# Expert layer of a small diffusion backbone: the last tile of the GLU product taken weight by weight, and the ring handed over unit by unit

## Chip, cores and metric

The kernel runs on one core of one Trainium2 chip. The metric is the device time of one execution in microseconds (us); the median of several executions is compared. All operands are fp32.

## What is computed

One layer (DEPTH is 1) for 128 context tokens and 256 latent tokens of width 1024, three tiles of 128 tokens. Cut to what the change touches:

```python
# ssm_mixer, its end: y is (tokens, 1024), w_glu is (1024, 2048)
val, gate = jnp.split(jax.nn.gelu(y).astype(h.dtype) @ w_glu, 2, axis=-1)
m = val * jax.nn.sigmoid(gate)
# run_stream
x = x + g1 * m
h = rms_norm(x, p["norm_ffn"][i]) * (1 + sc2) + sh2
# moe: router of 16 experts, best group of 4, two best experts in it
scores = jax.nn.sigmoid((t @ router_w).astype(jnp.float32))
g = jnp.einsum("nd,edf->nef", t, w_gate)
u = jnp.einsum("nd,edf->nef", t, w_up)
a = jax.nn.silu(g) * u * combine[:, :, None].astype(t.dtype)
y = jnp.einsum("nef,efd->nd", a, w_down)
x = x + g2 * moe(h, ...)        # then one final rms_norm
```

## The kernel before

The engines run five instruction lists written by hand; each keeps its own order and waits on semaphores. The list of SyncE (SP) issues nearly all DMAs.

**The ring.** The tile `ring` has 12 slots ("units") of 1 MB. Slots 0 to 7 later hold the gate and up weights of one expert (128 of the 1024 rows each), slots 8 to 11 its down weights (256 rows each). Before that, slots 4 to 11 hold `w_glu`, 128 rows in each slot (`load_glu`), slot 2 holds `yT_lat`, the transposed latent activations, and slots 0, 1 and 3 hold inputs of stages that end with the transposes counted by `pe_yT`.

**The GLU product** ("linear unit") is made in six parts m = 0 to 5 (`glu_part`, L1005): token tile t = m // 2, output half m % 2, and for each part `val` and `gate` in two PSUM banks (`GLU_BANK`). A part is 16 matmuls 128x512, which the trace shows as 32 records. Parts 0 and 1 are the context tile, 2 and 3 the first latent tile, 4 and 5 the second (last) one. Each part sums over eight slots, in the order of k = 4 to 7, then 0 to 3.

**After a part**: ScalarE takes the sigmoid (L700), VectorE multiplies, scales and adds to `x1` (L1416 to L1418), which counts `dve_x1`. After both parts of a tile ScalarE squares and sums (L707), takes a root (L709), and VectorE modulates to `h2` (L1333 to L1336). TensorE transposes `h2` (`transpose_h2`, L1040), ScalarE copies it out (`store_h2T`, L692), TensorE makes the 16 router logits of the tile (`logits`, L1049).

**Routing**: with all three tiles' logits, ScalarE takes the scores (L714) and VectorE chooses experts in some 40 small instructions (L1432 to L1495). TensorE sums ranks (L1070, L1071) and gathers the first expert's tokens (`gather_x`, L1082), VectorE copies them out (L1519, L1520).

**Experts**: a loop over 16. TensorE reads the expert's token count (L1128), branches to a body for 64 or for 96 tokens (L1129, L1131), multiplies by gate and up (L1096, a record per pass, 128 of them for 64 tokens and 192 for 96), gathers the next expert's tokens (L1082), transposes (L1108) and multiplies by down (L1118). Every slot is counted free in `unit_free` once read, and SP at once issues the same slot's load for the next expert (L368, L374). The last expert stands outside the loop. GpSimd scatters slot lists (L465) and each expert's output rows (L491).

**What sets the order around the change.** SP loads slots 0 and 1 for expert 0 after `pe_yT` 6, and then waits for all twelve counts of `pe_glu`, two per part, before it issues slots 2 to 11:

```python
            sp.wait_ge(pe_yT, 6)
            for u in range(2):
                load_unit(u, 0)
            sp.wait_ge(pe_glu, 12)
            for u in range(2, NU):
                load_unit(u, 0)
            sp.wait_ge(dve_x1, 6)
```

TensorE makes parts 2, 3 and 4, transposes tile 0 of `h2` into the two banks that part 5 then takes, waits for ScalarE's copies of it (`act_h2T` 2), and makes part 5.

Of the kernel before, what the change touches and what calls it, by code (L numbers as in the profile page):

```python
# [41 lines left out]
P = 128  # L42
D = 1024
KT = D // P
# [23 lines left out]
NU = 12  # L68
# [8 lines left out]
GLU_BANK = (2, 4, 0, 6, 2, 4)  # L77
# [4 lines left out]
def build(nc, x_prompt, x_sample, c, state_re, state_im, c_ctx, norm_mix, norm_ffn, w_ada, b_ada,  # L82
# [7 lines left out]
    with ctx:  # L90
        def sb(name, shape, dt=F32):
            return ctx.enter_context(nc.sbuf_tensor(name, shape, dt))

        def sem(name):
            return ctx.enter_context(nc.semaphore(name))


        ring = sb("ring", [P, NU, UNIT])
# [39 lines left out]
        yT_lat = ring[:, 2, :].rearrange("p (k t) -> p k t", k=KT)  # L138
# [18 lines left out]
        def cut(region, n):  # L157
            a = region[:, off[0]:off[0] + n]
            off[0] += n
            return a  # L160
        braw = cut(sreg, 2 * DG * GS).rearrange("p (r g h) -> p r g h", r=2, g=DG)
        craw = cut(sreg, 2 * DG * GS).rearrange("p (r g h) -> p r g h", r=2, g=DG)
        part = cut(sreg, GP * L * GS).rearrange("p (g k h) -> p g k h", k=L, h=GS)
# [53 lines left out]
        ps = [ctx.enter_context(nc.psum_tensor(f"ps{i}", [P, 512], F32)) for i in range(8)]  # L217
# [15 lines left out]
        pe_tr, pe_ada, pe_bc, pe_w, pe_cols, pe_hT, pe_u, pe_uT, pe_k, pe_p, pe_y, pe_fin, pe_yT = (  # L233
            sem(n) for n in ("pe_tr", "pe_ada", "pe_bc", "pe_w", "pe_cols", "pe_hT", "pe_u", "pe_uT",
                             "pe_k", "pe_p", "pe_y", "pe_fin", "pe_yT"))
        pe_inside = sem("pe_inside")
        act_ada, ld_glu_hi, ld_x_ctx, ld_mod_ctx = (sem(n) for n in ("act_ada", "ld_glu_hi", "ld_x_ctx", "ld_mod_ctx"))
        act_xs, act_lat, dve_rs, dve_cols, dve_ctx, act_v0 = (sem(n) for n in (
            "act_xs", "act_lat", "dve_rs", "dve_cols", "dve_ctx", "act_v0"))
        pe_glu, pe_h2T, pe_logit, pe_pos = (sem(n) for n in (  # L240
            "pe_glu", "pe_h2T", "pe_logit", "pe_pos"))
# [3 lines left out]
        act_yT, act_sig, act_h2T, act_score, act_fin, act_h0 = (sem(n) for n in (  # L245
            "act_yT", "act_sig", "act_h2T", "act_score", "act_fin", "act_h0"))
# [6 lines left out]
        dve_scan, dve_x1, dve_h2, dve_mask, dve_slot, dve_cmax, dve_x2, dve_out = (sem(n) for n in (  # L253
            "dve_scan", "dve_x1", "dve_h2", "dve_mask", "dve_slot", "dve_cmax", "dve_x2", "dve_out"))
# [23 lines left out]
        def of_half(i):  # L278
            return ident[:, :].rearrange("p (b i o) -> p i b o", i=2, o=2)[:, i]
# [7 lines left out]
        def _(sp):  # L287
# [23 lines left out]
            for n in range(KT, 3 * KT):  # L311
                b, k = divmod(n, KT)
# [52 lines left out]
            def load_unit(u, e):  # L365
                if u < KT:
                    for h, w in enumerate((w_gate, w_up)):
                        sp.dma_start(ring[:, u, h * D:(h + 1) * D],  # L368
                                     w[0, bass.ds(e, 1), u * P:(u + 1) * P, :].rearrange("a p n -> (a p) n")
                                     ).then_inc(ld_unit[u], 16)  # L370
                else:
                    for h in range(2):
                        k = 2 * (u - KT) + h
                        sp.dma_start(ring[:, u, h * D:(h + 1) * D],  # L374
                                     w_down[0, bass.ds(e, 1), k * P:(k + 1) * P, :].rearrange("a p n -> (a p) n")
                                     ).then_inc(ld_unit[u], 16)

            sp.wait_ge(pe_yT, 6)
            for u in range(2):
                load_unit(u, 0)  # L380
            sp.wait_ge(pe_glu, 12)
            for u in range(2, NU):
                load_unit(u, 0)
            sp.wait_ge(dve_x1, 6)
            for cond in range(2):
# [132 lines left out]
        def _(act):  # L518
# [51 lines left out]
            for m in range(2 * NT):  # L570
                t, k0 = m // 2, 4 * (m % 2)
# [116 lines left out]
            def store_h2T(t):  # L688
                for m in (2 * t, 2 * t + 1):
                    k0 = 4 * (m % 2)  # L690
                    act.wait_ge(pe_h2T, m + 1)
                    act.activation(h2T[:, k0:k0 + 4, t * P:(t + 1) * P],  # L692
                                   ps[(0 if t == 1 else 4) + m % 2][:, :].rearrange("p (k n) -> p k n", k=4), ACT.Copy
                                   ).then_inc(act_h2T, 1)
            for t in range(NT):
                for m in (2 * t, 2 * t + 1):
                    act.wait_ge(pe_glu, 2 * m + 2)
                    if m:
                        act.wait_ge(dve_x1, m)
                    act.activation(sig, ps[GLU_BANK[m] + 1][:, :], ACT.Sigmoid).then_inc(act_sig, 1)  # L700
                    if m == 4:
                        store_h2T(1)

                act.wait_ge(dve_x1, 2 * t + 2)
                if t:
                    act.wait_ge(act_sq, NT + t)
                act.activation(yrow, x1[:, t, :], ACT.Square, accum_out=stat[:, t:t + 1]).then_inc(act_sq, 1)  # L707
                act.wait_ge(dve_ms, 2 + t)
                act.activation(stat[:, 4 + t:5 + t], stat[:, 4 + t:5 + t], ACT.Sqrt).then_inc(act_rt, 1)  # L709
                if t == 1:  # L710
                    store_h2T(0)
            store_h2T(2)
            act.wait_ge(pe_logit, NT)
            act.activation(route[:, 0], ps[6][:, 0:NT * NE].rearrange("p (t e) -> p t e", t=NT), ACT.Sigmoid  # L714
# [43 lines left out]
        def _(pe):  # L758
# [20 lines left out]
            for i in range(2):  # L779
# [3 lines left out]
                for n, rows_in in enumerate((lnat[:, 0, :], lnat[:, 1, :], dtexp)):  # L783
                    last = pe.matmul(ps[7][a, n * DG:(n + 1) * DG], rows_in, of_half(i), start=True, stop=True)
# [37 lines left out]
            for i in range(2):  # L822
                last = pe.transpose(ps[3][:, 8 * i:8 * i + 8], drow[:, P * i:P * i + P], ident[0:8, 0:8])
# [8 lines left out]
            for q in range(4):  # L832
                last = pe.transpose(ps[3][:, q * P:(q + 1) * P], ada[:, 0, q * P:(q + 1) * P], ident[:])
# [46 lines left out]
            for m in range(8):  # L880
                if m >= 4:
                    pe.wait_ge(act_uT if m % 2 == 0 else dve_uT, (m - 4) // 2 + (1 if m % 2 == 0 else 2))
                for g in range(4 * m, 4 * m + 4):
                    src = u_c[0:C, 2 * g:2 * g + 2, :, :].rearrange("p i j h -> p (i j h)")
                    last = pe.transpose(ps[4 + m % 4][:, (g % 4) * C:(g % 4 + 1) * C], src, ident[0:C, 0:C])
# [6 lines left out]
            for m in range(0, 32, 2):  # L892
# [4 lines left out]
                for bi in range(2):  # L897
                    for r in range(2):
                        c0 = (2 * r + bi) * CX
                        for o in range(2):  # L900
                            a = slice(64 * o, 64 * o + 64)
                            for i in range(2):
                                g = 2 * (b0 + bi) + i
                                last = pe.matmul(ps[m % 8 + o][64 * i:64 * i + 64, c0:c0 + CX], pt[a, d, g, r, :],
                                                 uT[a, g, :], start=True, stop=True)
# [29 lines left out]
            def lat_bank(f, i):  # L935
                return ps[6 * f + i]
# [4 lines left out]
            def y_inside(bank_of, blocks, first_col, cols):  # L941
                for n, b in enumerate(blocks):
                    for i in range(2):
                        g = 2 * b + i
                        for o in range(2):
                            a = slice(64 * o, 64 * o + 64)
                            last = pe.matmul(y_out(bank_of(i), i, n, o, cols), t_of[a, g % 4, g // 4, :],
                                             uT[a, g, first_col:first_col + cols],
                                             start=(n == 0), stop=False, skip_group_check=True)
                return last  # L950
# [15 lines left out]
            def y_channels(k, bank, col, cols, y_of):  # L966
                for t in range(L):
                    for q in range(4):
                        last = pe.matmul(bank[32 * q:32 * q + 32, col + t * cols:col + (t + 1) * cols], pick[:, t, :],
                                         y_of(q % 2, 2 * k + q // 2), start=True, stop=True)  # L970
                return last
# [20 lines left out]
            for k in range(KT):  # L992
                last = y_channels(k, ps[2 + k // 4], (k % 4) * P, CC, lambda i, b: y_ctx[:, i, b, :])
# [23 lines left out]
            for f in range(2):  # L1017
                last = y_inside(lambda i: lat_bank(f, i), range(8 * f, 8 * f + 8), LAT0, CL)
# [5 lines left out]
            for f in range(2):  # L1024
                pe.wait_ge(act_gelu, 4 + 2 * f)
                for k in range(4 * f, 4 * f + 4):
                    last = y_channels(k, lat_bank(f, k % 4 // 2), (k % 2) * 256, CL,
                                      lambda i, b: y_lat[:, b // 8, i, b % 8, :])
# [4 lines left out]
            def transpose_h2(t):  # L1033
                pe.wait_ge(dve_h2, t + 1)
                for m in (2 * t, 2 * t + 1):
                    k0 = 4 * (m % 2)
                    if m >= 2:
                        pe.wait_ge(act_h2T, m - 1)
                    for k in range(k0, k0 + 4):
                        last = pe.transpose(ps[(0 if t == 1 else 4) + m % 2][:, (k % 4) * P:(k % 4 + 1) * P],  # L1040
                                            h2[:, t, k * P:(k + 1) * P], ident[:])
                    last.then_inc(pe_h2T, 1)

            def logits(t):
# [4 lines left out]
                    last = pe.matmul(ps[6][:, t * NE:(t + 1) * NE], h2T[:, k, t * P:(t + 1) * P], rw[:, k, :],  # L1049
                                     start=(k == 0), stop=(k == KT - 1))  # L1050
                last.then_inc(pe_logit, 1)
            for m in range(2, 6):
                if m >= 4:
                    pe.wait_ge(dve_x1, m - 3)
                if m == 5:
                    pe.wait_ge(act_h2T, 2)
                glu_part(m, tuple(range(4, KT)) + tuple(range(4)))
                if m == 4:
                    pe.wait_ge(dve_x1, 2)
                    transpose_h2(0)  # L1060
            pe.wait_ge(dve_x1, 4)
            logits(0)
            transpose_h2(1)
# [7 lines left out]
            last = pe.matmul(ps[7][:, 0:NT * NE], tri[:, 0, :], route[:, 20].rearrange("p t e -> p (t e)"),  # L1071
                             start=False, stop=True, skip_group_check=True)
# [537 lines left out]
```

## Time and profile before

| | |
|---|---|
| median of 3 runs | 886.0 us |
| all runs | 883.28, 886.0, 888.7 us |
| profiled execution, device time | 887.96 us |
| its span, first to last instruction | 886.3 us |
| mean granted TensorE clock | 0.916 |
| busy: TensorE, VectorE, ScalarE, GpSimd | 743.7, 300.4, 184.4, 63.6 us |
| moved by DMA | 259.34 MB, mean 293 GB/s |

The device time of the profiled execution is 1.66 us above its span. Views are given in microseconds from the span's start. A timeline row has start, duration, engine, line, operation, output and inputs, count, and in brackets how long the engine was idle before it and what released it ("issue" means that nothing the profile records was waited for). PE is TensorE, PEld its weight loads, PEldq its sequencer, SPq the DMA issues of SyncE.

### The profile page before, as it was taken

What the parts mean: (1) busy time and instruction counts of PE and PEld (TensorE: products, weight loads), DVE (VectorE), ACT (ScalarE), POOL (GpSimd) and SP (SyncE); (2) the same over time, 40 slices, a digit from 0 to 9 for tenths busy, and PEclk for the clock granted to TensorE, in tenths of its full rate; (3) what the DMA queues carried; (4) which work ended last, traced back from release to release, by engine and by line L of the source; (5) the groups of instructions that cost most, each with busy time, mean ns of one, the idle gap of its engine ahead of it and who ended that gap; (6) DMA issues with size and microseconds to landing.
All of it is one profiled execution on the core that took longest, in us unless ns stands there. A gap on an engine that the chain in (4) does not pass through costs nothing.

```text
span 886.3 us, 22538 instructions
## 1 busy us (share of the span) xinstructions
PE 743.7 (84%) x9579; PEld 415.3 (47%) x9580; DVE 300.4 (34%) x858; ACT 184.4 (21%) x386; POOL 63.6 (7%) x98
## 2 busy tenths in 40 slices
PE   5699776598969975899999999999999999999730
PEld 5355452094554445355545545544544554455220
DVE  3889789993004225021111111201201111120116
ACT  3553332010022211021121021201101112120113
POOL 1000003800010000200000000000000000000000
PEclk9899896657999985999999999999999999999985
DMA  8900439930018049599999999999998999999914
GB/s 347 397 3 2 190 138 403 332 132 3 26 33 287 1 153 368 192 391 412 410 411 410 409 410 410 410 410 403 411 411 318 413 410 410 410 410 410 385 56 169
DMA packets 70022, 259.34 MB, mean 293 GB/s; under 512 B 10728, under 2 KB 10776, under 8 KB 65864
## 3 DMA queue, kind: packets, MB, share of 16 engines
q1 hardware_dynamic: 66968, 254.02, 72.9%
q0 software_dynamic: 1632, 3.20, 1.0%
q10 hardware_dynamic: 1360, 1.19, 0.6%
q8 instruction: 51, 0.84, 0.4%
q14 instruction: 11, 0.09, 0.0%
HBM read 252.49 MB, written 6.29 MB: 292 GB/s over the span
## 4 chain that ended last, share of the span: by engine, by line
issue 53%; DVE 3%; POOL 2%; POOLq 1%; DMA 1%; ACT 0%; SPq 0%; DVEq 0%
POOL y_scratch L491 1%; POOLq L509 1%; DMA a4r<-slot_list 1%; POOL slot_list L465 1%; DMA ring<-y_scratch 0%; DVE ring L1574 0%; DVE sreg L1563 0%; DVE sreg L1564 0%; DVE sreg L1565 0%; POOL pool_tick L479 0%; DMA y_scratch<-vreg,sidx 0%; POOL sidx L484 0%; ACT sreg L746 0%; POOLq L508 0%; POOLq L497 0%
## 5 line engine op out<-in xcount | busy, mean ns | idle before, releaser
L1096 PE MATMUL ps<-ring,vreg 128*32 128x512 f32 x2240 | 246.7, 599 | 14.5 <-issue 14.2
L1096 PEld LDWEIGHTS ps<-ring,vreg 128*32 128x32 f32 x2240 | 74.6, 111 | 179.5 <-issue 179.5
L1118 PE MATMUL ps<-ring,vreg 128*32 128x256 f32 x2240 | 124.2, 380 | 17.0 <-ACT vreg L725 17.0
L1118 PEld LDWEIGHTS ps<-ring,vreg 128*32 128x32 f32 x2240 | 81.3, 110 | 56.1 <-issue 16.3
L1082 PEld LDWEIGHTS ps<-vreg,sreg 128*128 128x128 f32 x768 | 89.7, 197 | 14.2 <-issue 12.6
L1082 PE MATMUL ps<-vreg,sreg 128*128 128x96 f32 x768 | 92.3, 282 | 1.5 <-DVE vreg L1495 1.5
L1525 DVE TENSOR_TENSOR vreg<-vreg,ps 128x256 f32<-128x256 f32 x48 | 17.3, 417 | 224.8 <-ACT vreg L720 224.8
L1005 PE MATMUL ps<-ring 128*128 128x512 f32 x192 | 86.2, 611 | 2.2 <-ACT vreg L692 0.8
L1535 DVE COPY vreg<-ps 32x256 f32<-32x256 f32 x96 | 40.7, 424 | 132.3 <-PE ps L1118 129.8
L732 ACT ACTIVATE vreg<-ps 32x256 f32<-32x256 f32 x96 | 35.8, 373 | 131.5 <-PE ps L1118 129.5
L1005 PEld LDWEIGHTS ps<-ring 128*128 128x128 f32 x192 | 37.4, 196 | 49.1 <-issue 47.5
L720 ACT ACTIVATE vreg<-ps 128x256 f32<-128x256 f32 x48 | 15.0, 384 | 211.7 <-PE ps L1096 211.7
L864 PE MATMUL ps<-ring,sreg 128*128 128x512 f32 x96 | 44.7, 621 | 2.7 <-DVE sreg L1318 2.7
L1398 DVE TENSOR_TENSOR sreg<-sreg,scan_t 128x128 f32<-128x128 f32 x190 | 46.3, 284 | 1.1
L769 PE MATMUL ps<-ring,silu_c 128*32 128x512 f32 x192 | 32.4, 749 | 14.7 <-DMA ring<-in_w_ada 12.1
L431 POOL COPY ring<-ident 128x64 f32<-128x64 f32 x2 | 27.2, 13618 | 143.7 <-PE ps L929 143.6
L479 POOL TENSOR_TENSOR pool_tick<-ident 1x1 f32<-1x1 f32 x32 | 5.9, 183 | 440.5 <-DVE vreg L1535 355.4
L1416 DVE TENSOR_TENSOR vreg<-vreg,ps 128x512 f32<-128x512 f32 x6 | 4.1, 688 | 95.9 <-DMA sreg<-in_x_prompt 60.1
L1519 DVE COPY vreg<-ps 128x480 f32<-128x480 f32 x16 | 10.5, 657 | 65.6 <-PE ps L1082 65.6
L864 PEld LDWEIGHTS ps<-ring,sreg 128*128 128x128 f32 x96 | 18.6, 198 | 25.2 <-issue 25.0
L961 PE MATMUL ps<-sreg,vreg 64*64 64x32 f32 (+1 forms) x1024 | 25.5, 272 | 4.9 <-issue 4.4
L1390 DVE TENSOR_TENSOR scan_t<-a4r,sreg 128x128 f32<-128x128 f32 x95 | 27.0, 284 | 1.1
(255 smaller groups left out, 568.9 us busy)
## 6 DMA issues: line engine op xcount, KB each, us to landing
ring<-in_moe_w_gate SPq DMA_DIRECT2D x128, 512.0 KB, 12.4
ring<-in_moe_w_up SPq DMA_DIRECT2D x128, 512.0 KB, 14.0
ring<-in_moe_w_down SPq DMA_DIRECT2D x128, 512.0 KB, 10.5
ring<-in_w_ada SPq DMA_DIRECT2D x24, 1024.0 KB, 12.4
ring<-in_ssm_w_glu SPq DMA_DIRECT2D x8, 1024.0 KB, 11.8
ring<-in_ssm_w_in SPq DMA_DIRECT2D x8, 512.0 KB, 21.5
ring<-y_scratch SPq DMA_DIRECT2D x6, 512.0 KB, 5.9
tmat<-ada_rows SPq DMA_DIRECT2D x4, 512.0 KB, 10.8
```

The costliest lines, as they stand in the source:

```text
L431: pool.tensor_copy(pick[:, :, 16 * i:16 * i + 16], ident[:, 64 * i:64 * i + 64].rearrange("p (t h) -> p t h", h=GS)).then_inc(pool_pick, 1)
L732: act.activation(yrow[32 * t:32 * t + 32, 256 * j:256 * j + 256], src, ACT.Copy).then_inc(y_ev, 1)
L769: last = pe.matmul(ps[ADA_BANK[b]][32 * j:32 * j + 32, :], silu_c[:, k, :], src[:, j * 512:(j + 1) * 512], start=(n == 0), stop=(k == KT - 1),
L864: last = pe.matmul(ps[4 + m % 4][:, :], hT[:, k, tile * P:(tile + 1) * P], win[:, k, half * 512:(half + 1) * 512], start=(k == 0), stop=(k ...
L961: last = pe.matmul(y_out(bank_of(i), i, n, o, cols), v, states_of(a, d, r, g, first_col - 1 + 2 * d, cols), start=False, stop=(d == 1 and ...
L1005: last = pe.matmul(ps[GLU_BANK[m] + part][:, :], lhs, ring[:, 4 + k, col:col + 512], start=(k == 4), stop=(k == 3))
L1082: last = pe.matmul(bank[:, col * CAP:(col + 1) * CAP], h2[:, t, k * P:(k + 1) * P], onehot[:, t, :], start=(t == 0), stop=(t == NT - 1))
L1096: last = pe.matmul(ps[t][32 * j:32 * j + 32, :], xgT[:, k, 32 * t:32 * t + 32], w[:, :, 256 * j:256 * j + 256], start=(k == 0), stop=(k == ...
L1118: last = pe.matmul(ps[3 + t // 2][32 * dj:32 * dj + 32, 256 * (t % 2):256 * (t % 2) + 256], aT[:, t, c2, 32 * j:32 * j + 32], ring[:, KT + ...
L1390: step(tt(tb[0], A4R, chunk_states(f[st] - 1, b[st] + 1, False), ALU.mult), False)
L1398: step(tt(to, to, tb, ALU.add), False)
L1535: cp(yrow[32 * t:32 * t + 32, 256 * j:256 * j + 256], src).then_inc(y_ev, 1)
```

## The change

Parts 2 and 3 stay as they are, and `h2` of tile 0 is now transposed between them. Parts 4 and 5 are made together: for every k the four products (both halves, `val` and `gate`) follow one another into banks 2, 3, 4 and 5, and after the four a new semaphore, `glu_free`, counts the slot of that k as read. SP loads slots 0, 1 and 3 after `pe_yT` 6, then slots 8, 9, 10, 11, 4, 5, 6, 7, each on its own count of `glu_free`, and slot 2 last. ScalarE waits for all eight counts before the sigmoids of parts 4 and 5, and copies tile 0 of the transposed `h2` right after the sigmoid of part 2.

```diff
-        pe_inside = sem("pe_inside")
+        pe_inside, glu_free = sem("pe_inside"), sem("glu_free")
...
             sp.wait_ge(pe_yT, 6)
-            for u in range(2):
+            for u in (0, 1, 3):
                 load_unit(u, 0)
-            sp.wait_ge(pe_glu, 12)
-            for u in range(2, NU):
+            for n, u in enumerate((8, 9, 10, 11, 4, 5, 6, 7, 2)):
+                sp.wait_ge(glu_free, min(n + 1, KT))
                 load_unit(u, 0)
...
                 for m in (2 * t, 2 * t + 1):
-                    act.wait_ge(pe_glu, 2 * m + 2)
+                    if m < 4:
+                        act.wait_ge(pe_glu, 2 * m + 2)
+                    else:
+                        act.wait_ge(glu_free, KT)
                     if m:
                         act.wait_ge(dve_x1, m)
                     act.activation(sig, ps[GLU_BANK[m] + 1][:, :], ACT.Sigmoid).then_inc(act_sig, 1)
+                    if m == 2:
+                        store_h2T(0)
                     if m == 4:
                         store_h2T(1)
...
-                if t == 1:
-                    store_h2T(0)
...
-            for m in range(2, 6):
-                if m >= 4:
-                    pe.wait_ge(dve_x1, m - 3)
-                if m == 5:
-                    pe.wait_ge(act_h2T, 2)
+            for m in range(2, 4):
                 glu_part(m, tuple(range(4, KT)) + tuple(range(4)))
-                if m == 4:
+                if m == 2:
                     pe.wait_ge(dve_x1, 2)
                     transpose_h2(0)
+            pe.wait_ge(act_h2T, 2)
+            for k in tuple(range(4, KT)) + tuple(range(4)):
+                for m in (4, 5):
+                    for part in range(2):
+                        col = part * D + (m % 2) * 512
+                        last = pe.matmul(ps[GLU_BANK[m] + part][:, :], yT_lat[:, k, P:2 * P],
+                                         ring[:, 4 + k, col:col + 512], start=(k == 4), stop=(k == 3))
+                last.then_inc(glu_free, 1)
             pe.wait_ge(dve_x1, 4)
```

TensorE, from part 2 of the GLU product to the transposes of `h2` of tile 1 (128x512 into `ps` is the product, 128x128 a transpose, 128x16 the logits), before:

```order
L1005 MATMUL ps<-ring 128x512 [waits act_yT]
L1005 MATMUL ps<-ring 128x512 x31
L1005 MATMUL ps<-ring 128x512 [waits dve_x1]
L1005 MATMUL ps<-ring 128x512 x15
L1040 MATMUL ps<-ident,sreg 128x128 [waits dve_h2,dve_x1]
L1040 MATMUL ps<-ident,sreg 128x128 x7
L1005 MATMUL ps<-ring 128x512 [waits act_h2T,dve_x1]
L1005 MATMUL ps<-ring 128x512 x15
L1049 MATMUL ps<-sreg,vreg 128x16 [waits act_h2T,ld_route,dve_x1]
L1049 MATMUL ps<-sreg,vreg 128x16 x7
L1040 MATMUL ps<-ident,sreg 128x128 [waits act_h2T,dve_h2]
```

and with the change (L1008, L1065, L1043 and L1052 are the same statements in the longer file):

```order
L1008 MATMUL ps<-ring 128x512 [waits act_yT]
L1008 MATMUL ps<-ring 128x512 x15
L1043 MATMUL ps<-ident,sreg 128x128 [waits dve_h2,dve_x1]
L1043 MATMUL ps<-ident,sreg 128x128 x7
L1008 MATMUL ps<-ring 128x512 x16
L1065 MATMUL ps<-ring 128x512 [waits act_h2T]
L1065 MATMUL ps<-ring 128x512 x31
L1052 MATMUL ps<-sreg,vreg 128x16 [waits act_h2T,ld_route,dve_x1]
L1052 MATMUL ps<-sreg,vreg 128x16 x7
L1043 MATMUL ps<-ident,sreg 128x128 [waits act_h2T,dve_h2]
```

The eight transposes moved ahead of part 3, 48 matmuls follow them where 16 did, and the count of every kind is the same.

ScalarE, from the sigmoid of part 3 to the square of tile 2 (128x512 from `ps` at L700 is a sigmoid, at L692 a copy of transposed `h2`), before:

```order
L700 ACTIVATE vreg<-ps 128x512 [waits dve_x1,pe_glu]
L707 ACTIVATE vreg,stat<-sreg 128x1024 [waits act_sq,dve_x1]
L709 ACT_TABLE_LOAD
L709 ACTIVATE stat<-stat 128x1 [waits dve_ms]
L692 ACTIVATE vreg<-ps 128x4x128 [waits pe_h2T] x2
L700 ACT_TABLE_LOAD [waits dve_x1]
L700 ACTIVATE vreg<-ps 128x512 [waits pe_glu]
L692 ACTIVATE vreg<-ps 128x4x128 [waits pe_h2T] x2
L700 ACTIVATE vreg<-ps 128x512 [waits dve_x1,pe_glu]
```

and with the change, from the sigmoid of part 2:

```order
L703 ACTIVATE vreg<-ps 128x512 [waits pe_glu]
L692 ACTIVATE vreg<-ps 128x4x128 [waits pe_h2T] x2
L703 ACTIVATE vreg<-ps 128x512 [waits dve_x1,pe_glu]
L712 ACTIVATE vreg,stat<-sreg 128x1024 [waits act_sq,dve_x1]
L714 ACT_TABLE_LOAD
L714 ACTIVATE stat<-stat 128x1 [waits dve_ms]
L703 ACT_TABLE_LOAD [waits dve_x1]
L703 ACTIVATE vreg<-ps 128x512 [waits glu_free]
L692 ACTIVATE vreg<-ps 128x4x128 [waits pe_h2T] x2
L703 ACTIVATE vreg<-ps 128x512 [waits dve_x1,glu_free]
```

The sigmoid of part 4 now waits for the end of the whole product; between it and the sigmoid of part 5 the two copies of tile 1 stand as before.

## Rows read from the trace of the kernel before

**Rows 1.** The page: span, and DMA rates in its 40 slices
```profile
span 886.3 us, 22538 instructions
...
GB/s 347 397 3 2 190 138 403 332 132 3 26 33 287 1 153 368 192 391 412 410 411 410 409 410 410 410 410 403 411 411 318 413 410 410 410 410 410 385 56 169
```

**Rows 2.** Timeline, TensorE: first product of experts 0, 1 and 15
```profile
360.91 15.64 PE L1096 MATMUL ps<-ring,vreg 128*32 128x512 f32 x128 [3.16 <-issue]
...
391.19 13.94 PE L1096 MATMUL ps<-ring,vreg 128*32 128x512 f32 x128 [0.41 <-issue]
...
826.95 15.26 PE L1096 MATMUL ps<-ring,vreg 128*32 128x512 f32 x128 [5.82 <-issue]
```

**Rows 3.** Instructions of L1129 by themselves, near 357 and near 820 (duration min/median/max in ns)
```profile
L1129 PEldq COMPARE_BRANCH  x1: 3729/3729/3729, 356.7 to 356.7; - x1
...
L1129 PEldq COMPARE_BRANCH  x1: 6118/6118/6118, 820.5 to 820.5; - x1
```

**Rows 4.** Windows: length, busy time by engine, granted clock, DMA share, GB/s
```profile
346.00:352.00 6.00, 3.69 (x16) 3.53 (x17) 5.17 (x29) 1.28 (x1) 0.00 (x0) 0.50 1.01 403
352.00:358.00 6.00, 5.75 (x38) 5.59 (x37) 0.45 (x3) 0.00 (x0) 3.88 (x4) 0.73 0.07 18
358.00:364.00 6.00, 3.09 (x20) 0.88 (x24) 1.18 (x3) 0.00 (x0) 2.13 (x4) 0.84 0.03 3
```

**Rows 5.** Timeline, SyncE's DMA issues, 278 to 364
```profile
280.67 0.42 SPq L368 DMA_DIRECT2D ring<-in_moe_w_up  x1
322.14 0.33 SPq L368 DMA_DIRECT2D ring<-in_moe_w_gate  x1
...
363.69 0.36 SPq L368 DMA_DIRECT2D ring<-in_moe_w_gate  x1
```

**Rows 6.** Timeline, TensorE, 264 to 358
```profile
264.96 41.47 PE L1005 MATMUL ps<-ring 128*128 128x512 f32 x96 [0.69 <-ACT ring L684]
306.27 1.04 PE L1040 MATMUL ps<-ident,sreg 128*128 128x128 f32 x8
308.13 13.97 PE L1005 MATMUL ps<-ring 128*128 128x512 f32 x32 [0.83 <-ACT vreg L692]
321.94 1.85 PE L1049 MATMUL ps<-sreg,vreg 128*128 128x16 f32 x16
...
333.86 1.97 PE L1040 MATMUL ps<-ident,sreg 128*128 128x128 f32 x8 [6.45 <-DVE sreg L1336]
...
346.80 0.69 PE L1070 MATMUL ps<-sreg 128*128 128x64 f32 x2 [6.69 <-DVE sreg L1477]
...
349.40 8.35 PE L1082 MATMUL ps<-vreg,sreg 128*128 128x96 f32 x48 [1.51 <-DVE vreg L1495]
```

**Rows 7.** Timeline, VectorE, around part 2 and at the first gather
```profile
278.26 0.68 DVE L1336 TENSOR_TENSOR sreg<-sreg 128x512 f32<-128x512 f32 x1
...
281.18 0.69 DVE L1418 TENSOR_TENSOR sreg<-sreg,vreg 128x512 f32<-128x512 f32 x1
...
358.37 0.45 DVE L1520 COPY vreg<-ps 128x288 f32<-128x288 f32 x1
```

**Rows 8.** Timeline, ScalarE: the sigmoids of parts 2, 3 and 5
```profile
279.00 0.60 ACT L700 ACTIVATE vreg<-ps 128x512 f32<-128x512 f32 x1 [1.73 <-PE ps L1005]
292.74 0.60 ACT L700 ACTIVATE vreg<-ps 128x512 f32<-128x512 f32 x1 [13.14 <-PE ps L1005]
...
325.29 0.60 ACT L700 ACTIVATE vreg<-ps 128x512 f32<-128x512 f32 x1
```

**Rows 9.** Windows of 1 us, columns as in rows 4
```profile
355.00:356.00 1.00, 1.00 (x10) 1.00 (x10) 0.00 (x0) 0.00 (x0) 0.69 (x2) 0.89 0.00 0
...
363.00:364.00 1.00, 1.00 (x8) 0.23 (x4) 0.00 (x0) 0.00 (x0) 0.09 (x1) 0.50 0.00 0
```

**Rows 10.** Timeline, TensorE: parts 0 and 1, and a warm gather inside the loop
```profile
205.65 30.80 PE L1005 MATMUL ps<-ring 128*128 128x512 f32 x64 [0.69 <-ACT ring L672]
...
405.06 5.60 PE L1082 MATMUL ps<-vreg,sreg 128*128 128x96 f32 x48
```

## The prediction

> **What bounds the kernel now.** I read the page first, then the timeline of TensorE, then DMA rates by window, then the waits between the GLU product and the first expert.
>
> The page gives the span and the DMA rate of each slice of 22 us [rows 1]. From the 18th slice to the 38th the rate is about 410 GB/s almost throughout. That invites the reading that the expert loop is paced by its weights, and that loads which start earlier end the kernel earlier. The timeline of TensorE says otherwise [rows 2]. Expert 1 begins after only 0.41 us of idle time. Expert 15 waits 5.82 us, yet not for data: the branch L1129 before it takes from 820.5 for 6118 ns, to 826.6, and the product starts at 826.95 [rows 2, 3]. So TensorE paces the loop and the loads, each released by a slot that TensorE has read, follow. In such a loop the end moves exactly as its start moves, 360.91.
>
> What sets that start? Not the weights. The rate is still 403 GB/s in 346 to 352 and 18 GB/s in 352 to 358 [rows 4]: all twelve slots, and the two rows of `ada_rows` behind them, have landed at about 352.2 at the latest, **8.7 us before the first expert**. And expert 1's loads can't start before expert 0 has read a slot: SP issues the first at 363.69 [rows 5]. The ring has no thirteenth slot, so an earlier load of expert 0 pulls nothing behind it. DMA simply stands idle from 352 to 364 [rows 4].
>
> The chain that does set the start runs: end of part 5 at 321.94, logits and transposes, sigmoid of part 5 (325.29), norm of tile 2, its transposes (333.86), logits, routing (ranks at 346.80), the gather (349.40, 8.35 us), VectorE's copies (to 358.82), and the branch of 3729 ns from 356.7 to 360.4 [rows 3, 6, 7, 8]. Each pause of TensorE in it names a releaser on ScalarE or VectorE, none a DMA.
>
> **The change part by part.**
>
> *Order of TensorE.* From 264.96 to 308.13, the start of part 5, there are 43.17 us: 96 records of the product (41.47 with the last one's tail), eight transposes (1.04) and 0.83 us of waiting for ScalarE's copies [rows 6]. The product's pace is (41.47 - 0.16)/96 = 0.430 us a record, and the eight transposes now stand behind part 2. The wait of 0.83 goes, since part 3 (32 x 0.430 = 13.8 us) lies between the transposes and the next user of their banks. What is late next: `h2` of tile 0 is complete at 278.26 + 0.68 = 278.94, and part 2 ends at 264.96 + 13.76 = 278.72 [rows 6, 7]. So a new wait of about 0.2 us appears; I bound it by 0 and 0.4. **Sum: -0.83 + 0.2 = -0.63 us.** The pace over these 96 records is even although loads ran beside the first of them, so I take 0.430 us for parts 4 and 5 as well: 64 records, as before, 27.5 us.
>
> *Sigmoid and `x1` of part 4.* They were done while part 5 ran and now start after it. The price, by part 2: sigmoid at 279.00, last add done at 281.18 + 0.69 = 281.87, so 2.9 us [rows 7, 8]. The cover: the sigmoid of part 5 came only 325.29 - 321.94 = 3.35 us after the product's end, because ScalarE first copied tile 1 of the transposes [rows 6, 8]. With 0.2 us from the product to ScalarE, `x1` of part 4 is there 3.1 us after the end, 0.25 us before it is wanted. Cost 0, and up to 0.3 if the margin is gone. Without the copies between them the sigmoid would slip by the part of the 2.9 us that they now hide.
>
> *`store_h2T(0)`* is 2 copies in the 13.14 us for which ScalarE waited ahead of the sigmoid of part 3 [rows 8]: 0.
>
> *One more unit early, slot 3.* Two DMA issues of SP behind 280.67 + 0.42; SP then waited until 322.14 [rows 5]. 0.
>
> *Ring by units.* Parts 4 and 5 run from about 293.8 to 321.3, a slot free every 4 x 2 x 0.430 = 3.4 us. A slot is 1.05 MB, 2.6 us at 410 GB/s [rows 1], so loads keep up; slots 7 and 2 are issued at about 321.5 and land by 329, where the last ones landed by 352. SP's nine waits hold back only the loads behind them and the two rows of `ada_rows` that the kernel's end reads. **This is the large movement, some 23 us, and it is worth 0**: the cover is the 8.7 us by which the loads were early already. What it may give indirectly is less traffic beside the routing chain. The nearest rows are the two branches: 3729 ns with DMA idle, 6118 ns at full rate [rows 3, 4], 2.4 us apart. The one before expert 0 falls into idle DMA before and after, so the gain is bounded by 0 and 2.4, and I take 0, as no pause in the chain is left unexplained.
>
> *The clock.* TensorE is granted 0.50 where the first gather begins and 0.89 in 355 to 356; it falls to 0.50 again in 363 to 364, after the pause at 358 to 361 [rows 6, 9]. A gather inside the loop takes 5.60 us [rows 10], so this one may gain 2.75 us (5.60 against 8.35) or lose as much (11.2). The first product of expert 0 takes 15.64 against 13.94 [rows 2], so 1.7 more either way. Nothing in the change steers this; it goes into the range.
>
> Sum: -0.63, rounded to **-0.6 us**. The span becomes 885.7 and the profiled execution's own time 887.96 - 0.6 = 887.3; that execution lay 2.0 above the median of 886.0, so against the median I forecast **885.4 us**.
>
> **The rivals.** 0.5% of this kernel is 4.4 us; the runs shown, 883.28 to 888.7, lie up to 0.3% from their median, so 0.5% is about what a measurement can tell from no change.
>
> *Faster: the early loads do shorten the chain.* For it: 23 us of full-rate traffic leave a stretch in which TensorE, ScalarE and VectorE run new code once. The Trainium skill, page "Runtime: NRT & Kernel Launch", section "Instruction fetch mechanics", says that code is fetched by DMA and that a taken branch outside the loaded pages waits for such a fetch; rows 3 agree. The price is one hidden fetch at 2.4 us, giving -3.0 in all; two, or one with a warm gather (2.75), give -5.4 to -5.8, so about 880.4. Against it: each pause from 322 to 358 has a named releaser [rows 6], and the branch itself is met with DMA idle. Chance 0.11.
>
> *Slower: the clock falls while parts 4 and 5 go round four banks.* Place: the 64 records from 293.8. Before, the eight matmuls of a bank followed one another; now the bank changes with each matmul. If TensorE paused a little at each change and its clock were halved for a stretch, each record there would cost 0.43 more. All 64 would cost 27.5; the change is slower by 4.4 from (4.4 + 0.6)/0.43 = 12 records on. Taking 20 such records gives +8.0 us, 894.0. The Trainium skill, page "TensorE: Matmul & The Clock Gate", section "A second HAM failure mode: psum-queue depth-cycling", describes exactly this: a kernel that cycles through PSUM banks at N = 512 idles often enough for the clock to oscillate, which would make the result about that 894.0 instead of 885.4. Against it: a cold start of parts 0 and 1 cost 30.80 for 64 records [rows 10], 3.3 over 27.5, and the clock came back by itself; the weight loads run ahead, and the expert product walks over banks too, at 13.94 for 128 records [rows 2]. Chance 0.04.
>
> *Slower: nothing hides part 4.* If the margin of 0.25 us fails and copies come late, the end moves by at most 2.9 - 0.6 = +2.3, 888.3: still within 0.5%. It needs the cold clock on top (2.75) to pass it. Chance of that pair 0.03.
>
> *The change doesn't do what it says.* If SP meets a busy queue, slots are loaded as late as before. Since loads have 8.7 us to spare, the time is the same 885.4; it belongs to my forecast.
>
> **How the numbers follow.** Forecast within 0.5%: 0.82. Faster: 0.11. Slower: 0.04 + 0.03 = 0.07. For the range I go down from 885.4 by a warm gather (2.75) with 0.6 for the scatter of a median, to 882.0, and up by a cold one with what part 4 may cost (2.75 + 0.3) and 0.5, to 889.0. That leaves out the tails of the two named rivals.
>
> **What would show it.** Right: in the trace after, no `w_down` load issued later than some 310, DMA silent from about 332 to 363, expert 0 starting at about 360.3, the loop as long as before (826.95 - 360.91 = 466.0 us from expert 0's product to expert 15's), no pause of 0.83 us ahead of part 5, the sigmoid of part 5 some 3.3 us after the end of the product. Wrong: expert 0 before 358 with the same chain shorter in its pieces (traffic mattered), any granted clock under 1.0 between 294 and 321 (bank cycling), or a loop whose length changes, which would mean that the ring's lead does matter and that TensorE doesn't pace it alone.

## The result, and the profile after

| | before | with the change |
|---|---|---|
| median | 886.19 us (4 runs) | 900.2 us (4 runs) |
| range of the runs | 883.28 to 888.7 | 897.75 to 903.76 |
| profiled execution, time and span | 887.96, 886.3 | 901.68, 900.0 |
| mean granted clock | 0.916 | 0.906 |

The change makes the kernel slower: ratio 1.0154, 95% interval 1.0114 to 1.0194. The forecast was 885.4 and no change.

The page of the changed kernel, the lines that answer to [rows 1], with the clock and the line of the instruction queue:

```profile
span 900.0 us, 22537 instructions
...
PEclk9999895657999976999999979999999999999875
...
GB/s 346 388 2 2 187 175 387 344 84 3 48 83 255 239 227 2 324 407 410 410 410 410 409 240 385 413 410 364 411 411 318 409 411 410 410 410 410 337 51 171
...
q8 instruction: 49, 0.80, 0.4%
```

The DMA traffic came earlier, as predicted (227 and 2 GB/s in the 15th and 16th slice, where 153 and 368 stood). But the 24th slice, 517 to 540, has 240 GB/s in the midst of the expert loop, where nothing was changed. The instruction count fell by one. Now the timeline of TensorE up to the first experts, against [rows 6] and [rows 2]:

```profile
263.65 14.00 PE L1008 MATMUL ps<-ring 128*128 128x512 f32 x32 [0.69 <-ACT ring L684]
277.85 1.06 PE L1043 MATMUL ps<-ident,sreg 128*128 128x128 f32 x8 [0.20 <-DVE sreg L1343]
278.75 13.90 PE L1008 MATMUL ps<-ring 128*128 128x512 f32 x32
292.48 27.63 PE L1065 MATMUL ps<-ring 128*128 128x512 f32 x64
319.95 1.85 PE L1052 MATMUL ps<-sreg,vreg 128*128 128x16 f32 x16
...
331.87 1.97 PE L1043 MATMUL ps<-ident,sreg 128*128 128x128 f32 x8 [5.62 <-DVE sreg L1343]
...
347.41 7.62 PE L1089 MATMUL ps<-vreg,sreg 128*128 128x96 f32 x48 [1.51 <-DVE vreg L1502]
358.48 15.63 PE L1103 MATMUL ps<-ring,vreg 128*32 128x512 f32 x128 [3.44 <-issue]
```

Up to here this is what was forecast. From the start of part 2 to the end of the product there are 319.95 - 263.65 = 56.30 us, where 321.94 - 264.96 = 56.98 stood: -0.68, for -0.63. From there to the transposes of tile 2 there are 11.92 us both times. Expert 0 starts 2.43 us earlier, of which 1.31 had been there before part 2, in code that the change doesn't touch. The rest, 0.44, is the first gather (7.62 us for 8.35) less a longer pause behind it (3.44 for 3.16).

The loss comes later. The same view, at the end of expert 4 (the first with 96 tokens) and at expert 15:

```profile
502.23 10.57 PE L1125 MATMUL ps<-ring,vreg 128*32 128x256 f32 x192 [0.74 <-ACT vreg L728]
524.00 16.48 PE L1103 MATMUL ps<-ring,vreg 128*32 128x512 f32 x128 [11.21 <-issue]
...
837.78 16.61 PE L1103 MATMUL ps<-ring,vreg 128*32 128x512 f32 x128 [5.70 <-issue]
...
857.07 8.66 PE L1125 MATMUL ps<-ring,vreg 128*32 128x256 f32 x128 [0.96 <-ACT vreg L728]
```

Before the change the same two steps of experts 4 and 5 read:

```profile
504.28 10.57 PE L1118 MATMUL ps<-ring,vreg 128*32 128x256 f32 x192 [0.74 <-ACT vreg L725]
515.57 13.94 PE L1096 MATMUL ps<-ring,vreg 128*32 128x512 f32 x128 [0.72 <-issue]
```

So TensorE stands for 11.21 us before expert 5, once, where it stood for 0.72, and the product behind it takes 16.48 instead of 13.94. The ledger of the spans, +13.7: start of expert 0, -2.43; experts 0 to 3, +0.38; expert 4 to expert 5, +10.48 (49.51 for 39.03); expert 5 to expert 15, +2.40; from there to the end of the last product, +2.89 (27.95 for 25.06), in which the clock was at half for longer (16.61 and 8.66, for 15.26 and 7.11).

Windows around the pause tell whether data or code was missing (length, busy time of PE, PEld, DVE, ACT, POOL, granted clock, DMA share, GB/s):

```profile
515.00:518.00 3.00, 0.00 (x0) 0.00 (x0) 0.61 (x2) 1.58 (x2) 1.13 (x2) 0.59 1.01 403
518.00:521.00 3.00, 0.00 (x0) 0.00 (x0) 0.00 (x0) 0.00 (x0) 0.00 (x0) 0.50 0.94 373
521.00:524.00 3.00, 0.00 (x0) 0.00 (x1) 0.00 (x0) 0.00 (x0) 0.36 (x2) 0.50 0.06 25
524.00:529.00 5.00, 5.00 (x24) 1.22 (x28) 0.00 (x0) 0.00 (x0) 0.00 (x0) 0.50 0.03 2
```

No weights are missing: the ring is full at 521 and DMA stops, while TensorE stands until 524. The clock is at 0.50 (1.2 GHz) after the standstill and until 529, which goes with the 2.5 us that the product behind it takes longer (16.48 for 13.94). What TensorE's sequencer does meanwhile is in the instructions of the branch over the small body (L1138 after, L1131 before), first after and then before:

```profile
L1138 PEldq COMPARE_BRANCH  x1: 5978/5978/5978, 511.3 to 511.3; - x1
```
```profile
L1131 PEldq COMPARE_BRANCH  x1: 218/218/218, 513.4 to 513.4; - x1
```

It takes 5978 ns for 218, about as long as the branch ahead of expert 15 [rows 3]. That is the first half of the standstill. The second half is at the loop's end, in two instructions that follow one another, the count (ALU_OP) and the closing branch (L1143 after, L1136 before), again first after and then before:

```profile
L1143 PEldq ALU_OP  x1: 36/36/36, 517.4 to 517.4; - x1
L1143 PEldq COMPARE_BRANCH  x1: 223/223/223, 522.3 to 522.3; - x1
```
```profile
L1136 PEldq ALU_OP  x1: 36/36/36, 513.7 to 513.7; - x1
L1136 PEldq COMPARE_BRANCH  x1: 222/222/222, 513.9 to 513.9; - x1
```

With the change the closing branch starts 4.8 us after the count has ended, in the kernel before 0.14 us after it. The jump back to the head itself is short (223 ns), and the next token count is read at 522.7, so the head was at hand.

The trace also holds the packets that bring code. Those of queue q8 are all of 16384 bytes. That they are TensorE's is a reading from their times: one falls into each long branch of TensorE. Their starts between 480 and 545, us from the span's start:

```
before           489.0  505.1  512.8         521.3  540.1
with the change  486.8  503.0  510.7  514.9  519.9
```

With the change two pieces are fetched during the standstill, at 514.9 and 519.9, one for each of its two halves. There are not more fetches in all: q8 brings 49 packets with the change and 51 before, where the pieces at 521.3, 540.1 and one at 613 come while TensorE works. What differs is that TensorE stands for two of them. That this is the cause is a reading, and it has rivals; the experiments decide.

### The profile page after: what moved, and what is told of

It reads as the page before. It is cut to its first block, busy times and chain, and to the rows that moved or that the text cites. A ratio compares the mean times of both kernels' runs of the same rounds, so it can differ in the third digit from the quotient of the medians.

```text
span 900.0 us, 22537 instructions
## 1 busy us (share of the span) xinstructions
PE 749.0 (83%) x9579; PEld 415.8 (46%) x9580; DVE 300.5 (33%) x858; ACT 184.5 (20%) x386; POOL 63.8 (7%) x98
## 4 chain that ended last, share of the span: by engine, by line
issue 55%; DVE 3%; POOL 2%; POOLq 1%; DMA 1%; ACT 0%; SPq 0%; DVEq 0%
POOL y_scratch L491 1%; POOLq L509 1%; POOL slot_list L465 1%; DMA ring<-y_scratch 0%; DVE ring L1581 0%; DVE sreg L1570 0%; DVE sreg L1571 0%; DVE sreg L1572 0%; POOL pool_tick L479 0%; DMA y_scratch<-vreg,sidx 0%; POOL sidx L484 0%; ACT sreg L749 0%; DMA a4r<-slot_list 0%; POOLq L508 0%; POOLq L497 0%
## 5 line engine op out<-in xcount | busy, mean ns | idle before, releaser
L1103 PE MATMUL ps<-ring,vreg 128*32 128x512 f32 x2240 | 250.5, 606 | 25.5 <-issue 25.3
L1008 PE MATMUL ps<-ring 128*128 128x512 f32 x128 | 58.3, 616 | 1.4 <-ACT ring L672 0.7
L1008 PEld LDWEIGHTS ps<-ring 128*128 128x128 f32 x128 | 25.0, 198 | 32.5 <-issue 30.8
L1526 DVE COPY vreg<-ps 128x480 f32<-128x480 f32 x16 | 10.5, 658 | 64.8 <-PE ps L1089 64.8
L1397 DVE TENSOR_TENSOR scan_t<-a4r,sreg 128x128 f32<-128x128 f32 x95 | 29.6, 312 | 1.1
L1398 DVE TENSOR_TENSOR scan_t<-a4i,sreg 128x128 f32<-128x128 f32 x95 | 29.5, 310 | 0.0
## 6 DMA issues: line engine op xcount, KB each, us to landing
ring<-in_ssm_w_glu SPq DMA_DIRECT2D x8, 1024.0 KB, 11.6
```

The lines of the kernel that those rows point to most:

```text
L1008: last = pe.matmul(ps[GLU_BANK[m] + part][:, :], lhs, ring[:, 4 + k, col:col + 512], start=(k == 4), stop=(k == 3))
L1103: last = pe.matmul(ps[t][32 * j:32 * j + 32, :], xgT[:, k, 32 * t:32 * t + 32], w[:, :, 256 * j:256 * j + 256], start=(k == 0), stop=(k == ...
L1397: step(tt(tb[0], A4R, chunk_states(f[st] - 1, b[st] + 1, False), ALU.mult), False)
L1398: step(tt(tb[1], A4I, chunk_states(f[st] - 1, b[st] + 1, True), ALU.mult), False)
```

## The experiments

**Theory A**: the pause is code. The change takes one wait instruction out of TensorE's list ahead of the loop (the trace has 58 semaphore records of its sequencer for 59, since part 5's wait for `dve_x1` beside that for `act_h2T` went), so the whole loop lies one instruction earlier against the edges of the pieces, and after the first large body the code at the loop's end has to be fetched. **Theory B**: the early loads upset the ring. **Theory C**: the product over four banks, or the clock.

### One instruction back, and one instruction away

```diff
+            pe.wait_ge(dve_x1, 3)
             pe.wait_ge(dve_x1, 4)
             logits(0)
```

> The changed kernel with one more wait on TensorE, for dve_x1 3, just ahead of the wait for dve_x1 4: it is always satisfied, and its only effect is that TensorE's list ahead of the expert loop has as many instructions as before the change (one 64-byte instruction more, 40 separate waits instead of 39). Theory A (where the expert loop's code lies: the pause of 11.2 us before expert 5 is the fetch of code that was no longer held): the pause is gone, L1138's 5978 ns falls to some 220 ns, and the time is 886.2 - 14 + 14 - 2 = about 884. Theory B (the early loads upset the ring) and theory C (the product over four banks, or the clock after it): nothing changes, about 900.

Measured: 889.14 us against 888.51 of the kernel before in the same session, ratio 1.0012 (0.9978 to 1.0045). The branch and the product at expert 5, in that kernel:

```profile
L1139 PEldq COMPARE_BRANCH  x1: 217/217/217, 515.2 to 515.2; - x1
```
```profile
517.43 13.94 PE L1104 MATMUL ps<-ring,vreg 128*32 128x512 f32 x128 [0.72 <-issue]
...
829.03 16.47 PE L1104 MATMUL ps<-ring,vreg 128*32 128x512 f32 x128 [5.75 <-issue]
```

A wait that never waits takes the whole loss away. It also shows what the change is worth with the loop at its old place: nothing that can be told from zero (the interval is -2.0 to +4.0 us, and the -0.6 of the forecast lies inside it). The reverse, in the kernel before:

```diff
             for m in range(2, 6):
-                if m >= 4:
+                if m == 4:
                     pe.wait_ge(dve_x1, m - 3)
```

> The kernel before the change with one redundant wait taken out of TensorE's list (for dve_x1 2 ahead of part 5, which the transposes ahead of it have already waited for). One instruction less ahead of the loop, as in the change, and nothing else. Theory A: a pause of 11 us before expert 5 appears in the kernel before, about 886.2 + 10.5 + up to 3 of half clock = 897 to 900. Theories B and C: 886.

Measured: 902.89 us, ratio 1.0203 (1.014 to 1.0266). The old order of the product and the old, late loads, and the pause is there:

```profile
L1131 PEldq COMPARE_BRANCH  x1: 6122/6122/6122, 512.8 to 512.8; - x1
```
```profile
525.90 16.40 PE L1096 MATMUL ps<-ring,vreg 128*32 128x512 f32 x128 [11.63 <-issue]
```

That is the whole slowdown, with nothing of the change in it but its missing instruction. B and C fall as causes of the pause.

### The early loads undone, in both places

```diff
             for n, u in enumerate((8, 9, 10, 11, 4, 5, 6, 7, 2)):
-                sp.wait_ge(glu_free, min(n + 1, KT))
+                sp.wait_ge(glu_free, KT)
                 load_unit(u, 0)
```

> The changed kernel with slots 8 to 11, 4 to 7 and 2 loaded only after all eight counts of glu_free, as late as before the change; TensorE's list is that of the change, to the instruction. Theory A: the pause stays, about 900, and the early loads prove worth nothing. Theory B: the pause goes, about 886. Theory C: 900, with no code fetch in the pause.

Measured: 899.74 us (ratio 1.0183, 1.0113 to 1.0252), with the pause (slot 3 is still loaded early in this kernel):

```profile
520.67 16.20 PE L1103 MATMUL ps<-ring,vreg 128*32 128x512 f32 x128 [11.62 <-issue]
```

The same edit on top of the one more wait, where the loop doesn't pause:

> one_more_wait with the nine slots of expert 0 loaded only after all eight counts of glu_free: the early loads alone are undone, at the place at which the loop does not pause. If the early loads are worth nothing, it is level with one_more_wait and with the kernel before, within 0.3%. If they are worth something that the pause hid, it is slower by that.

Measured: 886.01 against 885.96, ratio 0.9991 (0.9967 to 1.0014). With early loads (one_more_wait) the ratio was 1.0012. The two intervals overlap: the 17 us or so by which the weights come earlier (loads end about 10 us after the product with the change, 27 in these two kernels) are worth nothing that these runs can tell, as the 8.7 us to spare [rows 4] had said. In loads_late the windows show the traffic beside the routing chain again (columns as above), and the chain is not longer for it: from the transposes of tile 2 to the rank sums it takes 342.72 - 329.79 = 12.93 us there, and 344.81 - 331.87 = 12.94 with the change and its idle DMA.

```profile
334.00:340.00 6.00, 2.03 (x10) 1.93 (x10) 3.11 (x19) 0.21 (x1) 0.00 (x0) 0.50 1.03 410
340.00:346.00 6.00, 1.77 (x7) 1.61 (x8) 5.17 (x28) 0.06 (x1) 0.00 (x0) 0.50 0.89 354
```

### Other places

32 satisfied waits on TensorE ahead of the rank sums:

```diff
+            for i in range(64):
+                pe.wait_ge((act_p, dve_p, act_k, act_pt)[i % 4], 1 + i // 4)
             pe.wait_ge(dve_mask, 1)
```

(two of these share an instruction, so 64 make 32.)

> The changed kernel with 32 satisfied wait instructions on TensorE in its idle time before the rank sums, so that the loop's code lies 2 KB further on. Theory A says that the time depends on that place and on nothing else here: the pause is gone or elsewhere, and I take 884 as for one more instruction; the waits lie in 6.7 us of idle time and cost nothing. Theories B and C: 900.

Measured: 887.52, ratio 0.9991 (0.995 to 1.0032), no pause. Then 256 and 240 of them, spread over parts 2 to 5 (each `pass_by` is eight satisfied waits in four instructions, while any are left):

```diff
                     for k in half_k:
+                        if t:
+                            pass_by()
...
                         col = part * D + (m % 2) * 512
+                        pass_by()
```

> The changed kernel with 256 satisfied wait instructions (64 bytes each, 16384 bytes in all) spread over parts 2 to 5 on TensorE, where its sequencer is far ahead of the array. The trace shows code coming in pieces of 16384 bytes. If what decides is where the loop lies against the edges of such pieces (A1), this is the place of the change again: the pause of some 11 us before expert 5 is back, about 900. If it is some other place, or only the count of instructions before the loop (A2), no pause and about 887, as for one and 32 more.

> The same with 240 wait instructions: by A1 the place of 16 instructions earlier than the change. It tells on which side of the change the bad places lie: with the pause (about 900) the change sits at the end of a stretch of bad places, without it (about 887) it is one of few. I expect the pause, since one more removes it and one edge of a piece crossing one target is the simplest reading.

Measured: 899.41 (ratio 1.0146, 1.0101 to 1.0191) with 256, and 892.24 (1.0087, 1.0052 to 1.0121) with 240. The first products of expert 5, with 256 and with 240:

```profile
522.33 16.66 PE L1113 MATMUL ps<-ring,vreg 128*32 128x512 f32 x128 [11.02 <-issue]
```
```profile
518.26 16.10 PE L1113 MATMUL ps<-ring,vreg 128*32 128x512 f32 x128 [6.61 <-issue]
```

256 instructions further on the pause is back, within 0.2 us (11.02 for 11.21), so what matters is the place against the edges of the pieces (A1 of the expectation), not the number of instructions. One more packet of 16384 bytes comes there, 50 for 49, which makes a wait instruction 64 bytes. 16 instructions ahead of the change's place half of the pause is there: the branch over the small body takes 6099 ns, and the closing branch follows the count without delay:

```profile
L1153 PEldq ALU_OP  x1: 36/36/36, 516.4 to 516.4; - x1
L1153 PEldq COMPARE_BRANCH  x1: 238/238/238, 516.5 to 516.5; - x1
```

My expectation of the full pause there was wrong. The traces suggest where the edge lies. The step from the count to the closing branch takes 4.6 to 5.1 us after expert 4 in all four kernels at the change's place, and up to 0.5 us in some of their other passes, but 0.05 to 0.15 us at the other places with this order of the bodies. So at the change's place the edge of a piece very likely lies between these two instructions: the jump needs the piece ahead of the edge for one instruction and then the one behind it. 16 instructions earlier both stand in one piece. One instruction later the jump lands behind the edge; why that piece is then at hand isn't shown. Together:

| place of the loop, instructions from the change's | kernels | pause before expert 5 | ratio to before |
|---|---|---|---|
| -16 | plus_240 | 6.61 us | 1.0087 |
| 0 | the change, loads_late, plus_256, before_minus_wait | 11.0 to 11.6 | 1.0146 to 1.0203 |
| +1 | the kernel before, one_more_wait, loads_late_good_place | 0.72 | 1, 1.0012, 0.9991 |
| +32 | plus_32 | 0.64 | 0.9991 |

### The order of the two bodies

```diff
-                with pe.If(n > 64):
-                    expert(e, last_of_round, TT)
                 with pe.If(n <= 64):
                     expert(e, last_of_round, 2)
+                with pe.If(n > 64):
+                    expert(e, last_of_round, TT)
```

> The changed kernel with the two bodies of the expert loop in the other order: that for up to 64 tokens first, that for up to 96 behind it, so that the commoner case falls through, at the first expert and at the last. By theory A the branch of 3.7 to 4.0 us before expert 0 and that of 6.0 us before expert 15 are code fetches of a jump over the large body, and go: expert 0 starts some 2 us earlier (VectorE's copies then bind), the last some 5.5 us and 1 to 2 of half clock. The jump over the large body now comes at the end of expert 0, once, for up to 6 us, and the pause before expert 5 may stay or go. Together 900 - 8 + 5 = 897 with that pause, 884 without it. If these are no code fetches, nothing changes, 900.

> small_body_first with the 32 satisfied waits of plus_32: the same order at another place. If the order and not the place makes the difference, both are alike within 3 us; I expect 884, with the pauses of the first kernel with this order or without them.

Measured: 888.71 (ratio 1.0037, 1.0008 to 1.0065) and 883.3 (0.9983, 0.9954 to 1.0013). First products of experts 0, 1 and 15 in the first of them:

```profile
354.68 13.94 PE L1103 MATMUL ps<-ring,vreg 128*32 128x512 f32 x128 [1.39 <-DVE vreg L1527]
...
393.78 16.48 PE L1103 MATMUL ps<-ring,vreg 128*32 128x512 f32 x128 [10.93 <-issue]
...
826.88 13.94 PE L1103 MATMUL ps<-ring,vreg 128*32 128x512 f32 x128
```

Where the small body falls through, the pauses before experts 0 and 15 go, down to VectorE's copies and to nothing; the pause before expert 5 is gone too. But the jump over the large body at the end of expert 0 costs 10.93 us and 2.5 of clock, about twice what I had put down: 6204 ns for the branch, and again 4.5 us between the count and the closing branch, at the same place as in the change. With the 32 waits the second part is gone:

```profile
L1140 PEldq COMPARE_BRANCH  x1: 7333/7333/7333, 382.2 to 382.2; - x1
```
```profile
391.49 16.41 PE L1105 MATMUL ps<-ring,vreg 128*32 128x512 f32 x128 [7.76 <-issue]
```

So the place matters with this order too. I had expected the two kernels alike within 3 us, and they are 5.4 apart. The branch before expert 15 was therefore worth attacking alone, outside the loop:

```diff
-            expert_by_count(NE - 1, True)
+            n = pe.value_load(counts[0:1, NE - 1:NE], min_val=0, max_val=T)
+            with pe.If(n <= 64):
+                expert(NE - 1, True, 2)
+            with pe.If(n > 64):
+                expert(NE - 1, True, TT)
```

> The changed kernel with the one more wait of one_more_wait, and for the last expert alone, which stands outside the loop, the small body ahead of the large one. The loop's code and its place are those of one_more_wait. If the 6.0 us before expert 15 are the fetch of a jump over the large body, the pause falls from some 5.8 us to some 0.3 and its first product from 16.5 to 13.9 us, as small_body_first showed: 889.1 - 5.5 - 2.5 = about 881, 0.8% below one_more_wait and the kernel before. If it were a wait for weights (the rival reading of that pause), nothing changes.

> The kernel before the change with the same edit of its last expert and nothing else. By the same theory it gains the same 5.5 us and up to 2.5 of half clock, 0.6 to 0.9%, and stands level with last_small_first: the gain has nothing to do with the change.

Measured: 878.9 (ratio 0.9927, 0.9897 to 0.9957) and 879.3 (0.9926, 0.9902 to 0.995). Both are clearly below the kernel before, and level with each other, so this gain has nothing to do with the change. The end of the changed kernel with this edit:

```profile
808.53 7.11 PE L1126 MATMUL ps<-ring,vreg 128*32 128x256 f32 x128 [1.15 <-ACT vreg L728]
815.44 13.94 PE L1104 MATMUL ps<-ring,vreg 128*32 128x512 f32 x128
```

## Why the prediction was wrong

*What bounds the kernel*: right up to a point. TensorE paces the loop, and the end follows its start. What failed is the next step, "the end moves exactly as its start moves": it takes the loop's length as fixed, and the length depends on where the loop's code lies: from the product of expert 0 to that of expert 15 it was 466.04 us before and 479.30 with the change. The prediction had named a changed length as a sign of being wrong, and read it as the ring's lead or a TensorE that doesn't pace the loop alone. The sign came, but not for that reason: loads_late and loads_late_good_place changed the lead and left the time. I had read the branch of 6118 ns before expert 15 as code [rows 3] and still priced code only at the two places where the trace of before showed it.

*Order of TensorE*: the wait of 0.83 us that goes I counted as time and never as an instruction. Its companion, one wait instruction of 64 bytes, was the expensive part: +10.5 us at expert 5 and 2.5 of half clock behind it, against -0.68. (The +2.89 at expert 15 is the clock as well, but its first product also took 16.47 us in one_more_wait, so I don't lay it to the pause.) The listing of TensorE's order shows no separate wait instructions, but part 5's first matmul carried two names before and one after.

*The forecast terms*: -0.68 measured for -0.63. The new wait for `h2` was 0.20 for 0.2. The product at four banks kept 27.63 us for 64 records and a granted clock of 1.00 until 322, so the slower rival (a result of 894) had the right side by the wrong cause; the Trainium skill's section on psum-queue depth-cycling ("TensorE: Matmul & The Clock Gate"), which tells of a bf16 kernel where these products are fp32, has no counterpart in this trace. The sigmoid of part 5 came 323.29 - 319.95 = 3.34 us after the product, for 3.35. Early loads: 0 within the intervals, at both places of the loop.

*The clock*: the first gather gained 0.73 of the 2.75 that it might, and the first product of expert 0 nothing. What I left out is that a new standstill can bring a cold clock behind it: after the pause at expert 5 the granted clock was 0.50 for 5 us, at a price of 2.5 us.

*The faster rival* looked at the right thing, fetches of code, and only asked whether the change would save one. The same row bore the opposite: a branch that finds its target may cease to find it. A rival "the loop stands once or twice more for code", at 5 to 6 us each and 2.5 of clock, would have given 894 to 900. Whether the change would meet a bad place, the rows of before didn't tell; that it did was bad luck.

## What to carry to other kernels

Any edit of an engine's list moves all the code behind it; in a loop with two long bodies that cost two standstills of 5 to 6 us here, though the edit is a saved wait. So compare the long branches and the idle time before the first product of each pass before believing an effect of the edit itself, and test it once more with a satisfied wait added. Where a branch stands outside a loop, put the likelier body first: here, with at most 64 tokens for the last expert, that gave 0.7%. Inside the loop the same order gave nothing clear (1.0037 and 0.9983), since the saved jumps were paid for by one at the end of expert 0.

## What the runs showed of the hardware

One satisfied wait fewer ahead of the loop cost 14.4 us in the kernel before (888.51 to 902.89), one more took the changed one from a ratio of 1.0154 to 1.0012, and 256 of them brought the pause back. Code came in packets of 16384 bytes. The Trainium skill ("Runtime: NRT & Kernel Launch", "Instruction fetch mechanics") describes blocks of 16 KiB and a stall on a taken branch whose target is outside the loaded ones; the runs agree, with 3.3 to 4.1 us for the branch ahead of expert 0, where DMA is idle, and 6.0 to 6.2 us, once 7.3, where weights stream. It speaks of a window of two blocks, and there the runs differ: with the change no packet came on q8 from 519.9 to 834.9, ten passes of the loop over both bodies, though a pass over the small body alone has 632 records of TensorE, at 64 bytes each an estimate of 40 KB. So more than two pieces were kept. Which ones, and why a loop that has run four times over its small body loses its end during the first large one, at some places and not at others, stays open: no run here varied the size of the bodies.
